# Which projections are split into heads and rests beside the attention of a two-layer decoder trunk: the convolution's inputs and gates take the place of the gated queries and keys, and the work hung on them is dealt anew

## The chip, the cores and the metric

One core of a Trainium2 chip runs the whole program: TensorE (PE) for matrix products, VectorE (DVE), ScalarE (ACT) and GpSimd (POOL) for the rest, and SyncE (SP), which only issues transfers here. The time is microseconds (us) on the device from the first to the last instruction with what lies around them. The value for a kernel is the median of its runs. The trace is of one execution.

## The reference

Two layers over 512 tokens of 1024 numbers. A layer is a token mixer, a cross-attention into a memory of 256 rows, and a mixture of 16 experts (two for each token). The change touches the mixer alone. It projects the normalised rows by one matrix, and three groups of heads work on the pieces:

```
h = rms_norm(x, norm_mix[l]);  z = h @ w_in[l]
(g_q, g_k, g_v, g_lr, g_r, d_q, d_k, d_v, i_q, i_k, i_w, c_u) = split(z)
# gated linear attention: 4 heads, 48 wide keys, chunks with an exact decay inside
log_a = log_sigmoid(g_lr @ wa2 + ba) / 16;  b = cumsum(log_a) in the chunk
attn[t,s] = sum_d q[t,d] k[s,d] exp(b[t,d] - b[s,d])   (s <= t)
o = attn @ v + (q exp(b)) @ state;  state = exp(b_last) state + (k exp(b_last - b))^T v
# sparse attention: 6 heads, each query keeps its 128 best causal keys by an indexer's score
# convolution: a, g = split(c_u);  y = a * sigmoid(g);  y = causal depthwise conv, 31 taps;
#              channel LayerNorm, swish
x = x + concat(o_gla * silu(g_r), o_dsa, o_conv) @ w_out[l]
```

## The kernel before

**Projections.** The 3,000 odd columns of `w_in` are loaded in nine chunks (`CHUNKS`) into three slots of the arena. `JOBS` lists the projections in the order in which PE makes them; a job of kind "T" gives 128 outputs by 512 tokens, one of kind "tok" 128 tokens by 384 outputs, and each is made of 8 units, one for each 128 rows of the contraction. Chunk 1 and chunks 2 to 5 (`SPLIT`) are computed from heads and rests: ACT copies the weights, rounded to the fast format, into a head (`chunk_head`), POOL writes the remainder (`chunk_rest`), and PE makes three fast products for a unit (`split_project`, line 708) in place of one slow product in full precision (line 726; line 729 for the 384 wide ones). The rows of h are split in the same way once.

**The steps.** After the indexer, 24 steps follow (4 query tiles by 6 heads, `STEPS`). In step n PE turns the probabilities of step n (line 848, 1 to 4 blocks), makes the logits of the next two steps (839) and the values of the last two (859) in even steps, and then does a share of the other work: units of projections, the decayed chunk keys turned ("kt", 740), state updates ("upd", 748), outputs of the gated heads ("o", 761 and 763). `work_of` deals these from the end of the list of jobs before the steps: `LENGTH` holds a time for each kind of unit, `attention` one for the step's own products, and the dealer keeps each step to a common pace, with one pace for the first `GATED` steps and another to step 21.

**The softmax ring.** DVE's step n begins with the inverse of the sum (`sum_inverse(n)`, line 1212) and the masked logits of the next step (`masked(n+1)`, 1207). ACT's step n normalises the probabilities (`normalise(n)`, 1044), takes the exponentials of the next step (1037), copies the turned probabilities (`turned`, 1062), and then copies out each job that ended in the step (`evacuate`, 955; 946 for updates, 934 and 938 for outputs). PE's turn of step n+1 waits for `normalise(n+1)`, which stands behind those copies on ACT and behind `sum_inverse(n+1)` on DVE.

**Levels.** The gated heads' matrix inside a chunk of 128 tokens (`AT`) is built in seven levels v = 0 to 6 (blocks of 1 to 64) and a diagonal. For each level DVE forms the differences of b (`differences`, 1233), ACT their exponentials (`level_decays`, 1075 and 1076), DVE multiplies by the queries (`level_queries`, 1241) and POOL by the keys (`level_keys`, 1356), PE makes the products (`level_products`, 788), and DVE, or ACT from level 5 on, merges them into `AT` (`merge`, 1257; `merge_blocks`, 1054). The diagonal (`diagonals`, 772) takes queries times keys from the third of three buffers `lev`, so `differences(2)` waits for it, and `differences(v)` waits for the products of level v-3. `LEV0`, the first step of the levels, comes from the step in which the last gated key is done.

**Around them.** When the last keys or gates are there, `decay_to_end` (1262) and `factors` (1266, 1269) make the factors of the state. The convolution is 62 operations of DVE (`conv_tap`, 1221 to 1224), spread over steps `FIRST_TAP` to 21 by `taps_spread`, which evens out `vector_us(n)`, DVE's other work as it is planned; DVE also makes ten rounds of the last tile's selection in steps 0 to 4. ACT takes the Sigmoid of the gates behind the copy of the last one (line 958), for which it loads another table of functions and then loads the first again.

## Time and profile before

| | us |
|---|---|
| median of 3 runs (lowest, highest) | 1549.1 (1540.87, 1553.7) |
| the profiled execution | 1541.7 |
| its span | 1539.5 |
| PE busy, DVE busy, ACT busy, POOL busy | 1427.3, 1163.9, 909.9, 552.0 |
| steps of layer 0, first turn to last value | 128.3 to about 297 |
| steps of layer 1 | 892.7 to about 1061 |

The profiled execution lies 2.2 us over its span and 7.4 us below the median of the runs. The steps of the two layers take some 168 us each, 22% of the span together; the rest is the indexer, cross-attention and above all the experts. A PE that is busy is not a PE at its peak: its busy time says that products follow each other, and its granted clock stands beside it.

### The profile page before, as it was taken

To read this page: it belongs to the slowest core of one execution; us is meant where nothing else is said; L and a number is where in the kernel's file an instruction comes from. 1 tells how busy PE (TensorE), PEld (TensorE's weight loads), DVE (VectorE), ACT (ScalarE), POOL (GpSimd) and SP (SyncE) were. 2 spreads that over 40 slices of the span, in tenths; PEclk is the share of its full clock that TensorE was granted. 3 is DMA by queue.
4 is the path that set the end of the run, shared out by engine and by line. 5 is a ranking of instruction groups with operands and counts; after the bars stand their busy time and mean duration, and the time that the engine had idled before them with its cause. 6 is when DMAs were issued, how large, how long until landed. Compare 5 with 4: busy or idle time off the path is not lost.

```text
span 1539.5 us, 20216 instructions
## 1 busy us (share of the span) xinstructions
PE 1427.3 (93%) x6710; PEld 1034.8 (67%) x6710; DVE 1163.9 (76%) x1658; ACT 909.9 (59%) x1346; POOL 552.0 (36%) x240
## 2 busy tenths in 40 slices
PE   7999998899899999999889999888998999999996
PEld 4687554457577878777556875544675778887773
DVE  4696589333569999999757965894335899999997
ACT  5643344553447787788475524446435588887781
POOL 2342332060005555554532413220600066555544
PEclk9999999999989999999999999999999999999998
DMA  6241601311328999999651421013221499999995
GB/s 227 89 110 42 217 1 55 137 57 37 128 110 302 399 398 399 398 399 399 227 197 42 109 74 76 1 55 137 57 89 77 152 340 399 399 399 398 398 399 196
DMA packets 151482, 312.71 MB, mean 203 GB/s; under 512 B 33158, under 2 KB 46380, under 8 KB 151228
## 3 DMA queue, kind: packets, MB, share of 16 engines
q1 hardware_dynamic: 140300, 271.39, 48.8%
q0 software_dynamic: 6624, 24.12, 4.2%
q10 hardware_dynamic: 4496, 16.40, 2.6%
q8 instruction: 36, 0.59, 0.2%
q14 instruction: 26, 0.21, 0.0%
HBM read 287.76 MB, written 29.50 MB: 206 GB/s over the span
## 4 chain that ended last, share of the span: by engine, by line
PE 45%; DVE 25%; DMA 17%; ACT 7%; issue 5%; DVEq 1%; POOL 0%; SPq 0%; POOLq 0%; ACTq 0%
PE ps L708 12%; DMA arena<-in_w_down 12%; DVE rest_w_down L1421 7%; PE ps L726 5%; PE ps L1498 4%; DVE mixr L1224 3%; DMA arena<-in_w_gate 3%; DVE rest_w_up L1421 3%; PE ps L1520 3%; DVE rest_w_gate L1421 2%; ACT head_w_down L1416 2%; PE ps L815 2%; DVE xg_rest L1434 2%; PE ps L1614 2%; PE ps L859 1%
## 5 line engine op out<-in xcount | busy, mean ns | idle before, releaser
L2084 POOL TENSOR_TENSOR rest_w_down<-arena,head_w_down 128x2048 fp32r<-128x2048 f32 x30 | 184.9, 6165 | 199.3 <-ACT head_w_down L1416 199.3
L1421 DVE TENSOR_TENSOR rest_w_down<-arena,head_w_down 128x2048 fp32r<-128x2048 f32 x30 | 148.3, 4944 | 16.9 <-ACT head_w_down L1416 16.8
L1421 DVE TENSOR_TENSOR rest_w_gate<-arena,head_w_gate 128x2048 fp32r<-128x2048 f32 x64 | 145.8, 2279 | 0.1
L1421 DVE TENSOR_TENSOR rest_w_up<-arena,head_w_up 128x2048 fp32r<-128x2048 f32 x64 | 143.5, 2281 | 0.1
L1416 ACT ACTIVATE head_w_gate<-arena 128x2048 fp32r<-128x2048 f32 x60 | 114.8, 1920 | 45.2 <-DMA arena<-in_w_gate 45.2
L1416 ACT ACTIVATE head_w_down<-arena 128x2048 fp32r<-128x2048 f32 x60 | 115.3, 1927 | 38.1 <-DMA arena<-in_w_down 37.4
L1416 ACT ACTIVATE head_w_up<-arena 128x2048 fp32r<-128x2048 f32 x64 | 121.8, 1946 | 8.3 <-DMA arena<-in_w_up 8.2
L1405 PE MATMUL ps<-head_w_gate,xg_head 128*128 128x512 f32 x256 | 104.1, 407 | 5.1 <-DVE xg_rest L1434 3.7
L1395 PE MATMUL ps<-head_w_down,he_head 128*128 128x512 f32 x240 | 99.5, 415 | 7.3 <-DVE rest_w_down L1421 4.3
L726 PE MATMUL ps<-hT,arena 128*128 128x512 f32 x224 | 101.7, 598 | 0.1
L1224 DVE SCALAR_TENSOR_TENSOR mixr<-arena,cf,mixr 128x512 f32<-128x512 f32 x120 | 97.6, 813 | 4.3
L1407 PE MATMUL ps<-head_w_gate,xg_rest 128*128 128x512 f32 x256 | 100.1, 391 | 0.0
L1406 PE MATMUL ps<-rest_w_gate,xg_head 128*128 128x512 f32 x256 | 100.0, 391 | 0.0
L1405 PE MATMUL ps<-head_w_up,xg_head 128*128 128x512 f32 x256 | 99.7, 390 | 0.0
L1407 PE MATMUL ps<-head_w_up,xg_rest 128*128 128x512 f32 x256 | 99.7, 389 | 0.0
L1406 PE MATMUL ps<-rest_w_up,xg_head 128*128 128x512 f32 x256 | 99.6, 389 | 0.0
L1397 PE MATMUL ps<-head_w_down,he_rest 128*128 128x512 f32 x240 | 94.1, 392 | 0.0
L1396 PE MATMUL ps<-rest_w_down,he_head 128*128 128x512 f32 x240 | 93.8, 391 | 0.0
L708 PE MATMUL ps<-hT_head,w_rest 128*128 128x512 f32 x224 | 90.0, 402 | 0.0
L2031 POOL DMA_INDIRECT xg<-hrows,slot_tok x2 | 4.9, 2436 | 236.4 <-DVE slot_tok L2002 236.4
L2077 POOL DMA_INDIRECT xg<-hrows,idx x28 | 76.4, 2728 | 21.0 <-POOL idx L2090 21.0
L1428 ACT ACTIVATE xg_head<-ps,cf 128x128 fp32r<-128x128 f32 x256 | 69.1, 379 | 23.0 <-PE ps L1688 16.4
(373 smaller groups left out, 3496.1 us busy)
## 6 DMA issues: line engine op xcount, KB each, us to landing
arena<-in_w_gate SPq DMA_DIRECT2D x64, 1024.0 KB, 10.5
arena<-in_w_up SPq DMA_DIRECT2D x64, 1024.0 KB, 11.4
arena<-in_w_down SPq DMA_DIRECT2D x64, 1024.0 KB, 10.7
arena<-in_w_in SPq DMA_DIRECT2D x10, 1536.0 KB, 6.6
yrows<-yb ACTq DMA_DIRECT2D x30, 512.0 KB, 6.3
arena<-in_w_in SPq DMA_DIRECT2D x4, 2048.0 KB, 8.6
x<-in_x SPq DMA_DIRECT2D x8, 512.0 KB, 13.5
arena<-in_w_in SPq DMA_DIRECT2D x16, 256.0 KB, 4.8
```

Source lines behind the costliest of these rows:

```text
L708: last = nc.tensor.matmul(o, lhs, rhs, start=(c == 0 and a == 0), stop=(c == KD - 1 and a == 2))
L726: last = nc.tensor.matmul(ps[n % 2][0:width, :], w[:, c, col:col + width], hT[:, c, :], start=(c == 0), stop=(c == KD - 1))
L1224: do(nc.vector.scalar_tensor_tensor(o, cin[:, i, j:j + S], convw[:, i, j:j + 1], o, ALU.mult, ALU.add))
L1395: nc.tensor.matmul(out, ah, bh, start=(c == 0), stop=False)
L1396: nc.tensor.matmul(out, ah, bl, start=False, stop=False)
L1397: last = nc.tensor.matmul(out, al, bh, start=False, stop=(c == n - 1))
L1405: nc.tensor.matmul(ps[q][:, :], xh[:, c, :], wh[q][:, c, :], start=(c == 0), stop=False)
L1406: nc.tensor.matmul(ps[q][:, :], xh[:, c, :], wl[q][:, c, :], start=False, stop=False)
L1407: last = nc.tensor.matmul(ps[q][:, :], xl[:, c, :], wh[q][:, c, :], start=False, stop=(c == KD - 1))
L1416: nc.scalar.activation(wh[q][:, part(q, j), :], raw[q][:, part(q, j), :], ACT.Copy).then_inc(s_head[q], 1)
L1421: nc.vector.tensor_tensor(wl[q][:, c, :], raw[q][:, c, :], wh[q][:, c, :].bitcast(F32), ALU.subtract).then_inc(s_split[q], 1)
L2084: nc.gpsimd.tensor_tensor(wl[2][:, c, :], raw[2][:, c, :], wh[2][:, c, :].bitcast(F32), ALU.subtract)\
```

## The change

The chunk of the convolution's inputs `ca` and gates `cg` is now the fifth and the chunk of the gated queries and keys the sixth, so the first is computed from heads and rests and the second in full precision. The times in `LENGTH` are swapped with them; the first pace covers 4 jobs over the first `GATED` = 4 steps, and the first output may come at step 19, not 16. The levels begin at step 8 (before: 4), the factors at steps 10 and 11 (8 and 9), the taps at step 4 (10: planned from 8 on, the first one fell to 10). The third level buffer lies in `sq`, and the wait for the last level product ahead of the second gate of `gr` falls away. In a step, PE makes two units, then the level products, then the other units; before, all units came first. The diagonal now closes PE's step `LEV0 + 2` (before: `LEV0 + 1`), the level products of v stand in step `LEV0 + 3 + v` (before: `+ 2`) and their merges in `+ 4` (before: `+ 3`).

```diff
     [(0, COL["dv"], AH * AD)],
+    [(0, COL["ca"], 2 * CC)],
     [(64 * h, COL["gq"] + GK * h, 64) for h in range(GH)] + [(256 + 64 * h, COL["gk"] + GK * h, 64) for h in range(GH)],
-    [(0, COL["ca"], 2 * CC)],
     [(0, COL["gv"], GH * GV)],
...
             csq = view(arena, up + 6656, 2, S)
-            lev = [view(mixg[:, :, :].rearrange("p h s -> p (h s)"), 1024 * i, 2, S) for i in range(2)] + [view(arena, up + 5120, 2, S)]
+            lev = [view(mixg[:, :, :].rearrange("p h s -> p (h s)"), 1024 * i, 2, S) for i in range(2)] + [sq[:, :, :]]
             lrT = view(arena, up + 11776, S, rows=RANK)
...
             BEFORE_STEPS = len(JOBS)
-            JOBS += [(5, P * i, P, "T", "gq", i) for i in range(2)] + [(5, 2 * P + P * i, P, "T", "gk", i) for i in range(2)]
-            JOBS += [(6, P * i, P, "T", "ca", i) for i in range(2)] + [(6, CC + P * i, P, "T", "cg", i) for i in range(2)]
+            JOBS += [(5, P * i, P, "T", "ca", i) for i in range(2)] + [(5, CC + P * i, P, "T", "cg", i) for i in range(2)]
+            JOBS += [(6, P * i, P, "T", "gq", i) for i in range(2)] + [(6, 2 * P + P * i, P, "T", "gk", i) for i in range(2)]
             JOBS += [(7, 0, GH * GV, "tok", "gv", i) for i in range(NT)]
...
-            LENGTH = dict(gq=0.7, gk=0.7, ca=0.87, cg=0.87, gr=0.87, gv=0.65, kt=0.6, upd=0.7, o=1.5)
-            GATED, LAST_FILLED, FIRST_O = 8, 22, 16
+            LENGTH = dict(ca=0.7, cg=0.7, gq=0.87, gk=0.87, gr=0.87, gv=0.65, kt=0.6, upd=0.7, o=1.5)
+            GATED, LAST_FILLED, FIRST_O = 4, 22, 19
...
                 i, h = STEPS[n]
-                return 0.3 * (i + 1) + (0.9 if 5 <= n < NLEV + 7 else 0.0)
+                return 0.3 * (i + 1) + (0.9 if 10 <= n < NLEV + 12 else 0.0)
...
             first, then = range(GATED), range(GATED, LAST_FILLED)
-            paces = [filler(("gq", "gk", "ca", "cg"), first) / len(first), filler(("gv", "kt", "gr", "upd", "o"), then) / len(then)]
+            paces = [filler(("ca", "cg"), first) / len(first), filler(("gq", "gk", "gv", "kt", "gr", "upd", "o"), then) / len(then)]
             work_of, left, spent = [], list(parts), 0.0
...
             LEV_BANK = (2, 7)
-            LEV0 = step_of(done("gk") - 1) + 1 if done("gk") > BEFORE_STEPS else 0
+            LEV0 = step_of(done("gk") - 1) - 1
...
                 return 2 * v + 1
-            FACTORED = step_of(done("cg") - 1) + 1
+            FACTORED = step_of(done("gk") - 1) + 1
             STATES = step_of(done("upd") - 1) + 1
...
                 us = 0.55 + 0.13 * (i + 1)
-                us += 2.5 if n == LEV0 + 2 else 0.0
-                us += 1.5 if 0 <= n - LEV0 - 3 < BY_BLOCKS else 0.0
+                us += 2.5 if n == LEV0 + 3 else 0.0
+                us += 1.5 if 0 <= n - LEV0 - 4 < BY_BLOCKS else 0.0
                 us += 0.8 if 0 <= n - LEV0 - 2 < NLEV else 0.0
...
                 sp.dma_start(one_head, A["heads"].rearrange("p (n c) -> p n c", c=P)).then_inc(sN["wor_in"], 16)
-                sp.wait_ge(sN["proj_done"], done("gk"))
+                sp.wait_ge(sN["proj_done"], done("cg"))
                 for t in range(NT):
...
                         values(n - 2)
-                    for job, c in work_of[n]:
+                    for job, c in work_of[n][:2]:
                         work(job, c)
-                    if n == LEV0 + 1:
+                    if 0 <= n - LEV0 - 3 < NLEV:
+                        level_products(n - LEV0 - 3)
+                    for job, c in work_of[n][2:]:
+                        work(job, c)
+                    if n == LEV0 + 2:
                         diagonals()
-                    if 0 <= n - LEV0 - 2 < NLEV:
-                        level_products(n - LEV0 - 2)
                     if n == MEAN:
...
                         return
-                    if name == "gr" and i:
-                        act.wait_ge(sN["lev_mm"], NLEV + 1)
                     src = ps[n % 2][0:width, :] if kind == "T" else ps[n % 2][:, 0:384]
...
                         level_decays(n - LEV0 - 1)
-                    if BY_BLOCKS <= n - LEV0 - 3 < NLEV:
+                    if BY_BLOCKS <= n - LEV0 - 4 < NLEV:
                         for e in range(2):
-                            merge_blocks(n - LEV0 - 3, e)
+                            merge_blocks(n - LEV0 - 4, e)
                     if n == FACTORED:
...
                     if v == 0:
-                        dve.wait_ge(sN["proj_out"], done("gk"))
+                        dve.wait_ge(sN["proj_out"], done("cg"))
                     if v >= 2:
...
                 def decay_to_end():
-                    dve.wait_ge(sN["proj_out"], done("cg"))
+                    dve.wait_ge(sN["proj_out"], done("gk"))
                     bc = halves(b, P // 2)
...
                         masked(n + 1)
-                    if n == LEV0 + 2:
+                    if n == LEV0 + 3:
                         merge(0)
-                    if 0 <= n - LEV0 - 3 < BY_BLOCKS:
+                    if 0 <= n - LEV0 - 4 < BY_BLOCKS:
                         for e in range(2):
-                            merge(PRODUCTS.index((n - LEV0 - 3, e)))
+                            merge(PRODUCTS.index((n - LEV0 - 4, e)))
                     if 0 <= n - LEV0 - 2 < NLEV:
...
                                                toep[:, h, 2 * P - P * near:2 * P], ALU.add), "bm_done")
-                    if n == LEV0 + 1:
+                    if n == step_of(done("cg") - 1) + 3:
+                        gp.wait_ge(sN["proj_out"], done("cg"))
+                        do(nc.gpsimd.memset(AT, 0.0), "at_zero")
+                    if n == LEV0 + 3:
                         gp.wait_ge(sN["proj_out"], done("gk"))
-                        do(nc.gpsimd.memset(AT, 0.0), "at_zero")
                         do(nc.gpsimd.tensor_tensor(lev[2], gq, gk, ALU.mult), "lev_k")
-                    if 0 <= n - LEV0 - 3 < NLEV:
-                        level_keys(n - LEV0 - 3)
+                    if 0 <= n - LEV0 - 4 < NLEV:
+                        level_keys(n - LEV0 - 4)
                     if n == STATES - 1:
```

PE around the diagonal. Line 772 is the diagonal, 788 the products of a level, 848 a turn (it opens a step), 726 and 729 units. Before, steps 5 to 7:

```order
L726 MATMUL ps<-hT,arena 128x512 x7
L772 MATMUL ps<-cf,arena 128x2 x8
L848 MATMUL ps<-cf,scratch 128x128 x2
L839 MATMUL ps<-scratch 128x256 x2
L859 MATMUL ps<-scratch 64x128 x2
L726 MATMUL ps<-hT,arena 128x512 x6
L788 MATMUL ps<-mixg 128x64 x16
```

PE now, steps 10 to 12:

```order
L729 MATMUL ps<-arena,hT 128x384 x6
L772 MATMUL ps<-cf,sq 128x2 x8
L848 MATMUL ps<-cf,scratch 128x128 x2
L729 MATMUL ps<-arena,hT 128x384 x2
L788 MATMUL ps<-mixg 128x64 x16
L729 MATMUL ps<-arena,hT 128x384 x5
L848 MATMUL ps<-cf,scratch 128x128 x3
```

The products of level 0 stood behind six units of their step and stand behind two now, with five behind them.

DVE at the same place: 1241 are the queries of a level, 1262, 1266 and 1269 the factors, 1224 taps, 1233 differences, 1257 the merge of the diagonal (128x2048) and of blocks. Before, from the differences of level 1 (step 5) to those of level 2 (step 6):

```order
L1233 TENSOR_TENSOR mixg<-arena 128x1024
L1212 RECIPROCAL small<-small 128x1
L1207 ISA scratch,small<-ps,scratch 128x256
L1207 ISA small 128x1
L1257 COPY_PREDICATED arena<-cmask,ps 128x2048
L1241 TENSOR_TENSOR mixg<-arena,mixg 128x512
L1233 TENSOR_TENSOR arena<-arena 128x1024
```

DVE now, steps 10 and 11:

```order
L1262 TENSOR_TENSOR arena<-arena 128x1024
L1224 SCALAR_TENSOR_TENSOR mixr<-arena,cf,mixr 128x512 x2
L1233 TENSOR_TENSOR sq<-arena 128x1024
L1212 RECIPROCAL small<-small 128x1
L1207 ISA scratch,small<-ps,scratch 128x384
L1207 ISA small 128x1
L1257 COPY_PREDICATED arena<-cmask,ps 128x2048
L1241 TENSOR_TENSOR mixg<-arena,mixg 128x256x2
L1266 TENSOR_TENSOR arena<-arena 128x1024
L1268 COPY ebl<-arena 128x8
L1269 TENSOR_TENSOR arena<-arena 128x1024
L1233 TENSOR_TENSOR mixg<-arena 128x1024
```

The merge of the diagonal and the two factors now stand in one step, and the differences of level 2 ahead of them, in the diagonal's own step.

PE behind the last gate. Before, the end of step 7 (behind the last unit of `cg`):

```order
L729 MATMUL ps<-arena,hT 128x384
L788 MATMUL ps<-mixg 128x64 x16
L848 MATMUL ps<-cf,scratch 128x128 x2
L839 MATMUL ps<-scratch 128x256 x2
L859 MATMUL ps<-scratch 64x128 x4
```

PE now, the end of step 3 (the second 726 row opens the work of step 4):

```order
L726 MATMUL ps<-hT,arena 128x512
L848 MATMUL ps<-cf,scratch 128x128
L839 MATMUL ps<-scratch 128x256 x2
L859 MATMUL ps<-scratch 64x128 x2
L726 MATMUL ps<-hT,arena 128x512 x6
```

Between the last unit of the gates and the next turn there was a unit and a level's products; there is one unit now.

## Rows read from the trace of the kernel before

**Rows 1.** Busy time by stage (us and instructions of each engine, granted clock, DMA): the steps
```profile
128.00:297.00 169.00, 150.65 (x815) 93.34 (x816) 121.35 (x200) 71.70 (x160) 39.46 (x35) 0.97 0.25 89
893.00:1061.00 168.00, 149.97 (x813) 93.05 (x813) 120.70 (x198) 70.69 (x156) 39.06 (x35) 0.97 0.17 63
```

**Rows 2.** Waits of PE in the steps (total us, times, longest): layer 0, layer 1
```profile
PE ps L848 <- ACT scratch L1044: 18.7, 10, 3.7
...
PE ps L848 <- ACT scratch L1044: 17.0, 9, 3.7
```

**Rows 3.** The chain of waits, layer 0 (start, us, what)
```profile
137.78 6.84 PE ps L708 x30
...
205.47 1.24 DVE arena L1233
```

**Rows 4.** Timeline of PE (start, us, what): units and a level's products
```profile
160.25 6.28 PE L726 MATMUL ps<-hT,arena 128*128 128x512 f32 x14
193.45 3.49 PE L729 MATMUL ps<-arena,hT 128*128 128x384 f32 x10
214.16 2.00 PE L788 MATMUL ps<-mixg 48*128 48x64 f32 x32
```

**Rows 5.** Timeline of PE: turns that waited, in brackets how long, and products behind them
```profile
191.86 0.44 PE L848 MATMUL ps<-cf,scratch 128*128 128x128 f32 x2 [0.88 <-ACT scratch L1044]
207.48 0.69 PE L848 MATMUL ps<-cf,scratch 128*128 128x128 f32 x2 [3.08 <-ACT scratch L1044]
208.10 1.65 PE L839 MATMUL ps<-scratch 64*128 64x384 f32 x4
209.68 1.12 PE L859 MATMUL ps<-scratch 128*64 128x128 f32 x8
...
223.45 0.92 PE L839 MATMUL ps<-scratch 64*128 64x384 f32 x4
224.29 0.66 PE L859 MATMUL ps<-scratch 128*64 128x128 f32 x8
270.73 0.66 PE L848 MATMUL ps<-cf,scratch 128*128 128x128 f32 x4 [3.66 <-ACT scratch L1044]
282.27 0.66 PE L848 MATMUL ps<-cf,scratch 128*128 128x128 f32 x4 [1.30 <-ACT scratch L1044]
289.48 1.12 PE L848 MATMUL ps<-cf,scratch 128*128 128x128 f32 x4 [3.49 <-ACT scratch L1044]
```

**Rows 6.** Timeline of DVE: differences, merges, factors, three taps
```profile
156.93 3.25 DVE L1233 TENSOR_TENSOR mixg<-arena 128x1024 f32<-128x1024 f32 x1
...
174.42 2.47 DVE L1257 COPY_PREDICATED arena<-cmask,ps 128x2048 f32<-128x2048 uint8 x1 [7.17 <-PE ps L772]
183.00 2.65 DVE L1257 COPY_PREDICATED arena<-cmask,ps 128x512 f32<-128x512 uint8 x2 [2.34 <-PE ps L788]
201.22 2.18 DVE L1266 TENSOR_TENSOR arena<-arena 128x1024 f32<-128x1024 f32 x1
203.64 1.80 DVE L1269 TENSOR_TENSOR arena<-arena 128x1024 f32<-128x1024 f32 x1
218.51 3.56 DVE L1224 SCALAR_TENSOR_TENSOR mixr<-arena,cf,mixr 128x512 f32<-128x512 f32 x3
```

**Rows 7.** Timeline of ACT: normalising 128 and 512 wide, a table load, a copied update
```profile
142.42 0.39 ACT L1044 ACTIVATE scratch<-scratch,small 128x128 f32<-128x128 f32 x1
189.06 1.28 ACT L958 ACT_TABLE_LOAD   x1
190.35 1.06 ACT L958 ACTIVATE arena<-arena 128x1024 f32<-128x1024 f32 x1
250.79 0.66 ACT L946 ACTIVATE arena<-ps 48x192 f32<-48x192 f32 x2
281.50 0.71 ACT L1044 ACTIVATE scratch<-scratch,small 128x512 f32<-128x512 f32 x1
```

**Rows 8.** Timeline of POOL: queries times keys for the diagonal
```profile
156.70 2.40 POOL L1372 TENSOR_TENSOR arena<-arena 128x1024 f32<-128x1024 f32 x1
```

## The prediction

> **What bounds the kernel now.** I read the busy time by stage first, because the change touches only the 24 steps of each layer. They take 169 us in layer 0 and 168 us in layer 1, with PE busy for 150.7 and 150.0 of them, DVE for 121 and ACT for 72 [rows 1]. So a step ends with PE, and what a new order can win is PE's idle time. The waits of PE name it: its turns waited 18.7 us for ACT's normalised probabilities, ten times, and in layer 1 17.0 us, nine times; the first wait, of 1.7 us, lies before that window [rows 2]. That is the stock, 18.7 us a layer. The change adds and removes no unit, tap, level or transfer, so PE's 150 us stay.
>
> The chain of waits then says who stands behind ACT. Until step 8 the chain is PE itself, ten split units in 6.84 us [rows 3]. After that, up to step 17 of layer 0, it runs mostly through DVE, taps and differences such as the one of 1.24 us. The timeline has three kinds of late turn [rows 5]: behind the Sigmoid (0.88 us), behind DVE's step with the factors (3.08), and behind copies on ACT of jobs that ended with the step (3.66 and 3.49 behind two outputs, 1.30 behind one copy). After the stall of 3.08 us the products crawl: logits 1.65 against 0.92 us, values 1.12 against 0.66 at the same shapes. The granted clock has fallen to its lower level, 1.2 GHz, and the stall costs 1.2 us more.
>
> **The change, part by part, for one layer.**
>
> *Split chunk and full chunk swapped.* Four jobs are still split and four are not: 32 units of 0.68 us [rows 3] and 32 of 0.87 to 0.90 (seven in 6.28 [rows 4]). The loads swap with them, on the same slots' turns, and the first split unit is needed no earlier. Zero; DVE idles in steps 0 to 3 either way.
>
> *What goes.* The stalls that came from DVE in steps 9 to 17: 3.08 behind the factors, and, of the 18.7, the rest once 1.7, 0.88, 3.66, 1.30 and 3.49 are taken off too, 4.6 us in four turns. DVE now makes 28 taps in steps 4 to 9, where it had waited for PE, for instance 7.17 us for the diagonal [rows 6]. The Sigmoid's 0.88 goes as well. And with no stall of 3 us there, the 1.2 us of slow clock.
>
> *What comes on ACT.* Every turn stands behind `evacuate` of the jobs that ended in the step before. One copy of 512 with nothing behind it on PE costs 1.30 us [rows 5], of which 0.71 is normalising 512 wide; 128 wide it takes 0.39 [rows 7], so 1.0. By the new deal:
> - turn 1: `ca` 0 fills step 0 to its last unit, 1.0. Turns 2 and 3: one unit of 0.68 covers it, 0.3 each.
> - turn 4: the old stall of 0.88 came behind a cover of a unit and a level's products, 0.70 and 2.00 [rows 4], so the chain from the last gate to the turn is 3.5 us. The cover is one unit of 0.87 now: 2.6.
> - turn 8: `gk` 0 ends step 7, 1.1. Turn 13: a `gv` ends step 12 and a tile's output is copied too, 1.5.
> - turn 17: two updates end step 16, each copied in two pieces, 0.66 for the first [rows 7], 1.4; and level 6 on PE waits in step 17 for ACT's merge of level 5, 0.6.
> - turn 19: `gr` 1 ends step 18, with a tile's output, 1.7.
> - turn 20: the outputs' 3.66 now have two full units behind them, 1.7, and no tile's output, about 0.5: 1.4.
>
> Together 11.9 us.
>
> *What comes on DVE.* `differences(2)` overwrites the buffer that the diagonal reads. The diagonal stood in step 5 and the differences in DVE's step 6; now both stand in step 10, the diagonal last. Turn 11 therefore waits for the differences, 1.24 [rows 3], the inverse and the normalising, some 0.7 with their signals: 2.0. It is a new wait; queued behind it on DVE is the whole ring.
> Step 11 then holds the merge of the diagonal, 2.47, both factors, 2.18 and 1.80 [rows 6], queries and differences: a microsecond more than the old step of the factors, which had two merges of blocks instead. PE's step 11 is longer by 1.4 us, two units. So the old 3.08 comes back as 2.7; I take 3.0, because PE's level 0 must also wait for the merge in the middle of the step.
>
> *What stays.* 1.7 at the first turn and 3.49 behind the last outputs.
>
> *The sum.* 11.9 + 2.0 + 3.0 + 1.7 + 3.5 = 22.1 us of stalls against 18.7, less 1.2 of clock: +2.2 a layer, +4.4 us for both. Nothing behind the steps gives it back, since the experts start when the mixer has ended. That makes the profiled execution 1541.7 + 4.4 = 1546. The median of the runs stands 7.4 above that execution, so the forecast for the median is 1549.1 + 4.4 = **1553.5 us**.
>
> *Bounds.* The job-end terms are bounded by the row of 1.30 and by zero, where the dealt work runs a little long. The two DVE terms can vanish (no stall in steps 10 to 12: 5 a layer less, so 1543.5) or grow (second rival).
>
> *A table load.* The row shows 1.28 us for the load, and the Sigmoid begins 1.29 after its start, with no gap [rows 7]. The Trainium skill, ScalarE: Activation LUTs, section What ACT_TABLE_LOAD costs, counts a drain of about 1.38 us with every load. By that rule turn 4 would wait 4.0 instead of 2.6 us, and the sum would be +7. The trace disagrees with it here, and the chain of 3.5 us is measured with everything in it.
>
> **The rivals.** A measurement of this kernel tells about 1% (15 us) from no change.
>
> *The reordering pays in full (faster).* If the new deal leaves DVE ahead everywhere and the copies on ACT find a cover, only 1.7, 2.6, 1.4 and 3.5 are left, 9.2 us instead of 18.7, and the clock's 1.2 goes too: -10.7 a layer, 1549.1 - 21 = 1528. For it: the old chain is DVE from step 9 to 17, and PE's work moves exactly there. Against it: turn 21 before had a job that ended its step and waited 1.30, and the new deal has four such places more. Its half (the DVE terms alone vanish, and some copies) is 1540. I give 0.08 to a gain of over 1% and 0.15 to one that stays within it.
>
> *The level ring goes round DVE and PE in one step (slower).* Now `differences(v)` waits for the products of level v-3 in PE's same step, and those wait for DVE's merges of level v-2 in that step. The loop is opening 0.8, merges 2.65, products 2.0, differences 1.24 and signals 0.3, some 7.0 us [rows 4, 6], against PE's own 5.7 to 7.7 us in steps 11 to 15: even. What decides is POOL. Differences that took 1.24 took 3.25 beside queries times keys on POOL, 2.40 long [rows 6, 8], and three taps took 3.56 instead of 2.4 beside key products. If POOL's key product and bias fall into each of these five steps at 2 us or more, the loop takes 8 to 9.4, some 5 us more a layer beyond the stalls counted, and two stalls of 3 us bring the low clock back, 2.4: about +9.5 a layer, 1549.1 + 19 = 1568. From 1.5 us of overlap a step on it decides. For it: the rows; against it: the same POOL operations stood beside the same steps before, and the whole stock was 18.7. Chance 0.12.
> The Trainium skill, SBUF — State Buffer, section Who interferes with whom, says that such a DVE operation with two inputs in SBUF is blocked whole while GpSimd reads SBUF. By it a step's overlap is all of POOL's 2 us, and this rival is the likelier case; the row of 3.25 agrees with it.
>
> *The forecast:* stalls change hands, 1545 to 1560, 0.65.
>
> **The numbers.** Range 1538 to 1567: half of the faster rival below, nearly all of the slower one above, and the runs before spread from 8 us under to 5 over their median. Faster by over 1% 0.08; within 1% 0.80, which is the forecast's 0.65 and the smaller gain's 0.15; slower by over 1% 0.12.
>
> **What would show it.** In the changed profile: PE's busy time in the steps unchanged at 150 us a layer; the waits of the turns at 20 to 24 us; a turn about 2.5 us late behind the Sigmoid, some 30 us into the steps; a turn 2 us late directly behind line 772; no turn more than 1 us late in steps 5 to 7; taps in steps 4 to 9. Wrong would be: turns that wait under 14 us in total (the copies are covered), or over 28 with DVE idle for line 788 in steps 12 to 15 (the ring).

## The result, and the profile after

The changed kernel takes 1556.5 us (median of 7 runs, 1555.5 to 1561.7), against 1543.9 (7 runs, 1539.0 to 1553.7) of the kernel before on the same chip: ratio 1.0076, with 95% interval 1.0053 to 1.0100. That is within 1%, as forecast, and the median lies in the range. But the loss is 12.6 us, where 4.4 were forecast, and its cause was only half forecast. That the median comes within 3.0 us of the 1553.5 forecast is luck: the forecast stood on a median of 1549.1 from three runs, which seven runs put at 1543.9.

The profiled execution took 1556.5 us (span 1554.0), against 1541.7 (span 1539.5) before. Measured from the first turn of a layer to its last one (turn 0 to turn 23), the steps grew from 166.05 to 173.03 us in layer 0 and from 166.22 to 170.47 in layer 1, together 11.2 of the 14.5 us by which the span grew. Some 3.0 more lie behind the last turn of layer 1 (480.6 to 483.6), a stretch that the change doesn't touch and that varies from 481.5 to 485.9 us over the experiments below.

Busy time by stage, in the changed kernel: the steps of layer 0 and of layer 1 from first to last turn, then a short stretch of each (window, length, busy us and instructions of PE, PEld, DVE, ACT, POOL, granted clock, DMA share, GB/s).

```profile
129.00:302.00 173.00, 154.86 (x794) 94.44 (x795) 115.30 (x196) 68.82 (x155) 36.51 (x35) 0.94 0.23 84
899.90:1070.40 170.50, 151.92 (x795) 92.41 (x796) 115.33 (x196) 68.72 (x155) 36.53 (x35) 0.96 0.17 60
...
208.90:219.30 10.40, 10.05 (x43) 6.53 (x42) 10.09 (x12) 2.04 (x5) 2.00 (x2) 0.51 0.00 0
983.80:987.10 3.30, 3.30 (x6) 1.69 (x6) 3.16 (x6) 0.17 (x1) 0.00 (x0) 0.50 0.00 0
```

The same stretches of the kernel before, turn to turn.

```profile
128.30:294.40 166.10, 148.74 (x795) 91.87 (x796) 119.70 (x196) 69.57 (x155) 39.40 (x35) 0.97 0.24 87
892.70:1058.90 166.20, 148.86 (x795) 92.05 (x796) 119.61 (x196) 69.50 (x155) 39.36 (x35) 0.97 0.17 62
```

PE holds as many instructions as before and is busy for 6.1 us more in layer 0 and 3.1 in layer 1. Its idle time grew by only 0.8 and 1.2 (17.4 to 18.1 and to 18.6). So most of the loss is not waiting: the same products took longer, and the granted clock says why, 0.94 and 0.96 for 0.97. For 10.4 us of layer 0 it was 0.51, that is 1.2 GHz, while PE was 97% busy. The other runs agree with this one execution: over the whole span the granted clock was 0.964 to 0.968 in the seven runs of the changed kernel, and 0.967 to 0.976 in 25 runs of the kernel before.

The waits of PE in the steps of layer 0 of the changed kernel (total us, times, longest) answer to [rows 2].

```profile
PE ps L848 <- ACT scratch L1044: 18.5, 12, 3.5
PE ps L859 <- ACT scratch L1062: 0.7, 1, 0.7
PE ps L788 <- ACT arena L1054: 0.6, 1, 0.6
PE ps L788 <- DVE arena L1257: 0.3, 1, 0.3
```

The turns wait 18.5 us where they waited 18.7 before, turn 0's 1.69 included in both; the levels add 0.9. The timeline of PE in the changed kernel answers to [rows 5]: turns 1, 4, 11 and 22 with their waits in brackets, and what follows turns 4 and 11.

```profile
137.99 0.33 PE L848 MATMUL ps<-cf,scratch 128*128 128x128 f32 x1 [0.98 <-ACT scratch L1044]
160.33 0.33 PE L848 MATMUL ps<-cf,scratch 128*128 128x128 f32 x1 [2.49 <-ACT scratch L1044]
...
161.29 0.69 PE L859 MATMUL ps<-scratch 128*64 128x128 f32 x4
161.92 6.68 PE L726 MATMUL ps<-hT,arena 128*128 128x512 f32 x12
...
207.72 0.44 PE L848 MATMUL ps<-cf,scratch 128*128 128x128 f32 x2 [2.12 <-ACT scratch L1044]
207.99 1.89 PE L729 MATMUL ps<-arena,hT 128*128 128x384 f32 x4
210.23 3.68 PE L788 MATMUL ps<-mixg 48*128 48x64 f32 x32 [0.35 <-DVE arena L1257]
213.84 6.09 PE L729 MATMUL ps<-arena,hT 128*128 128x384 f32 x10
...
296.95 0.66 PE L848 MATMUL ps<-cf,scratch 128*128 128x128 f32 x4 [3.50 <-ACT scratch L1044]
```

A level's products take 3.68 us where they took 2.00 [rows 4], and five units of 384 (x10, each unit leaves two records) take 6.09 where they took 3.49. Step 11, from turn 11 to turn 12, is 12.05 us long in layer 0. In layer 1, behind the same stall, the clock is down for 3.3 us only, and only from 5 us behind turn 11 on: the level's products still take 2.00 us, the five units 5.19.

```profile
978.73 0.44 PE L848 MATMUL ps<-cf,scratch 128*128 128x128 f32 x2 [2.13 <-ACT scratch L1044]
981.24 2.00 PE L788 MATMUL ps<-mixg 48*128 48x64 f32 x32 [0.78 <-DVE arena L1257]
983.17 5.19 PE L729 MATMUL ps<-arena,hT 128*128 128x384 f32 x10
```

There step 11 is 9.46 us long.

### The profile page after: what moved, and what is told of

It is laid out like the page before. It is cut to its first block, busy times and chain, and to the rows that moved or that the text cites. A ratio compares the mean times of both kernels' runs of the same rounds, so it can differ in the third digit from the quotient of the medians.

```text
span 1554.0 us, 20214 instructions
## 1 busy us (share of the span) xinstructions
PE 1441.8 (93%) x6710; PEld 1042.2 (67%) x6710; DVE 1157.0 (74%) x1658; ACT 908.9 (58%) x1346; POOL 546.3 (35%) x240
## 4 chain that ended last, share of the span: by engine, by line
PE 50%; DVE 20%; DMA 16%; ACT 7%; issue 5%; POOL 1%; DVEq 1%; POOLq 0%; SPq 0%; ACTq 0%
DMA arena<-in_w_down 13%; PE ps L708 12%; DVE rest_w_down L1423 8%; PE ps L726 6%; PE ps L1500 4%; DVE rest_w_up L1423 3%; PE ps L729 3%; PE ps L1522 3%; DVE rest_w_gate L1423 2%; ACT head_w_down L1418 2%; PE ps L815 2%; PE ps L788 2%; PE ps L1616 2%; DVE xg_rest L1436 2%; DMA arena<-in_w_gate 1%
## 5 line engine op out<-in xcount | busy, mean ns | idle before, releaser
L726 PE MATMUL ps<-hT,arena 128*128 128x512 f32 x224 | 106.3, 614 | 0.0
L1367 POOL TENSOR_TENSOR scratch<-sel,toep 128x256 f32<-128x256 f32 (+1 forms) x48 | 40.6, 846 | 149.6 <-DVE small L1207 135.7
## 6 DMA issues: line engine op xcount, KB each, us to landing
arena<-in_w_gate SPq DMA_DIRECT2D x64, 1024.0 KB, 10.4
```

Of the source, the lines that this page charges most:

```text
L726: last = nc.tensor.matmul(ps[n % 2][0:width, :], w[:, c, col:col + width], hT[:, c, :], start=(c == 0), stop=(c == KD - 1))
```

## The experiments

Theory A in them: the waits come as forecast, and those ahead of turns 4 and 11 also drop TensorE's clock, which makes the loss. "Steps" is turn 0 to turn 23, layer 0 / layer 1, in the one profiled execution. Ratios are to the kernel before, with 95% interval. That kernel was run anew on the chip of each set: its median was 1547.7 us beside the first four experiments, 1545.5 beside the next four and 1549.1 beside the last two. So kernels of different sets are compared by their ratios, not by their medians.

| kernel | steps, us | median, us (runs) | ratio |
|---|---|---|---|
| before | 166.05 / 166.22 | 1543.9 (7) | 1 |
| changed | 173.03 / 170.47 | 1556.5 (7) | 1.0076 [1.0053, 1.0100] |
| fillers in two waits | 168.73 / 168.23 | 1549.6 (10) | 1.0012 [0.9989, 1.0034] |
| diagonal first | 168.86 / 168.95 | 1547.7 (10) | 1.0001 [0.9980, 1.0023] |
| Sigmoid later | 168.30 / 166.65 | 1546.8 (10) | 1.0001 [0.9978, 1.0024] |
| taps late | 178.93 / 173.52 | 1564.0 (4) | 1.0115 [1.0082, 1.0147] |
| both moves | 164.59 / 166.32 | 1542.2 (12) | 0.9978 [0.9963, 0.9994] |
| ends covered | 164.30 / 163.01 | 1535.4 (6) | 0.9940 [0.9921, 0.9959] |
| before, with fillers | 166.51 / 166.47 | 1544.7 (10) | 0.9981 [0.9965, 0.9996] |
| ends covered, fillers | 159.79 / 161.48 | 1530.4 (6) | 0.9902 [0.9882, 0.9921] |
| units first | 184.01 / 177.06 | 1568.6 (4) | 1.0169 [1.0114, 1.0224] |
| more fillers | 159.78 / 161.49 | 1532.4 (6) | 0.9909 [0.9873, 0.9946] |

**Fillers in two waits.** Products of constants, two each time (x4, two records each), whose results nobody reads, go into the waits of turns 4 and 11.

```diff
                 for n in range(NS):
+                    if n in (4, 11):
+                        idle_products(2)
                     turn(n)
```

> The changed kernel with two products of ones (0.87 us each at full clock) put ahead of the turns of steps 4 and 11 in both layers, into an unused bank; nothing else. Theory A (the lost time is TensorE's clock: a stall of 2.1 to 2.5 us drops it to 1.2 GHz, and 4 to 10 us of products behind it run at half speed): the fillers run inside the waits of 2.49 and 2.12 us, the granted clock stays at 1.0 in steps 4 and 11, step 4 shrinks from 8.1 to about 6.3 us, step 11 from 12.05 (layer 0) and 9.46 (layer 1) to about 8.5 with 1 to 1.5 us of the gain coming back as a wait of turn 12 for DVE. In sum 7 to 9 us of the span go, ratio to before about 1.001 to 1.003. Theory B (DVE and PE hold each other up in the level ring, the clock is only a symptom): the steps keep their lengths, since turn 12 waits for DVE as long as PE saved; under 4 us go, nearly all of it in step 4.

Timeline of PE in this kernel, turns 4 and 11 of layer 0 with what follows them.

```profile
156.67 1.89 PE L401 MATMUL ps<-ones 128*128 128x512 f32 x4
159.33 0.33 PE L848 MATMUL ps<-cf,scratch 128*128 128x128 f32 x1 [0.77 <-ACT scratch L1046]
...
160.22 0.44 PE L859 MATMUL ps<-scratch 128*64 128x128 f32 x4
...
202.85 1.97 PE L401 MATMUL ps<-ones 128*128 128x512 f32 x4
205.12 0.44 PE L848 MATMUL ps<-cf,scratch 128*128 128x128 f32 x2 [0.30 <-ACT scratch L1046]
207.63 2.00 PE L788 MATMUL ps<-mixg 48*128 48x64 f32 x32 [0.78 <-DVE arena L1259]
209.56 5.18 PE L729 MATMUL ps<-arena,hT 128*128 128x384 f32 x10
```

No turn comes earlier: steps 3 and 10, which hold the waits, are 8.48 and 9.69 us long as in the changed kernel (8.47 and 9.69). But the products behind turn 4 go at full speed (0.44 for 0.69) and step 4 takes 6.51 us instead of 8.11; step 11 takes 9.46 instead of 12.05, and 8.87 in layer 1. So 4.3 of the 7.0 us that layer 0 had lost, and 2.2 of layer 1's 4.3, are clock behind these two stalls, shown by taking the idleness away and leaving the delay. Together that is 6.5 us of steps, a little under the 7 to 9 expected: a fall of a few us remained in step 11 of layer 0 (5.18 for the five units), and in layer 1, where none did, turn 12 waited 0.94 us.

**Diagonal first.** The diagonal's products go ahead of the remaining units of PE's step, so that DVE's differences are done when turn 11 wants its probabilities.

```diff
+                    if n == LEV0 + 2:
+                        diagonals()
                     for job, c in work_of[n][2:]:
                         work(job, c)
-                    if n == LEV0 + 2:
-                        diagonals()
```

> The changed kernel with the diagonal put behind the first two units of its step 10 instead of behind all six. Theory A: differences of level 2 no longer wait for it, the stall of 2.12 us ahead of turn 11 goes and with it the low clock of step 11: step 10 from 9.69 to about 7.5, step 11 from 12.05 and 9.46 to 7.5 to 9 (it may wait for the merge of the diagonal less, and turn 12 for the factors more), about 3 to 6 us a layer, 6 to 11 in all, and the median comes to within 0.3% of before. Theory B: the 2.1 us reappear as a wait of turn 12 or of the products of level 0 behind DVE, whose step 11 holds 9.5 us of work in any case: 0 to 3 us in all.

The wait ahead of turn 11 is gone: step 10 takes 7.51 us for 9.69, step 11 takes 8.71 for 12.05. Steps 3 to 5, with the Sigmoid's stall in them, stayed at 8.47, 8.11 and 5.26. Of the 5.5 us gained there in layer 0, 1.3 went again in step 22, 6.35 us for 5.07, behind the same stall of 3.50. Now, at full clock, turn 12 waits 1.09 us and level 0's products 0.52, 1.6 together, where 3.0 had been forecast for these steps and 0.35 came in layer 0 of the changed kernel: there PE crawled and DVE caught up.

**Sigmoid later.** ACT's table load and Sigmoid, which stood in `evacuate` right behind the last gate, go behind `turned` of the step that follows, past the probabilities that turn 4 wants.

```diff
-                    if name == "cg" and i == 1:
-                        act.wait_ge(sN["proj_out"], n + 1)
-                        nc.scalar.activation(csig, csig, ACT.Sigmoid).then_inc(sN["cg_ready"], 1)
...
                     turned(n)
+                    if n == step_of(done("cg") - 1) + 1:
+                        act.wait_ge(sN["proj_out"], done("cg"))
+                        nc.scalar.activation(csig, csig, ACT.Sigmoid).then_inc(sN["cg_ready"], 1)
```

> The changed kernel with the Sigmoid of the gates moved on ACT from behind the copy of the last gate to behind the copy of the turned probabilities of step 4, so that the turn of step 4 doesn't stand behind it. Theory A: turn 4 waits 0.3 to 0.4 us (the copy of the last gate alone) instead of 2.49, the clock stays up in step 4 (8.1 to 6.3 us), the first taps start a few us later and are made up in steps 5 to 9: 4 us a layer, about 8 in all. Theory B: DVE waits longer for the gates, its taps run into step 10 and the levels, and half of the gain is lost there: 4 us or less in all.

Timeline of ACT in this kernel.

```profile
156.69 0.60 ACT L955 ACTIVATE arena<-ps 128x512 f32<-128x512 f32 x1 [4.51 <-PE ps L708]
157.18 0.39 ACT L1041 ACTIVATE scratch<-scratch,small 128x128 f32<-128x128 f32 x1
159.35 1.28 ACT L1083 ACT_TABLE_LOAD   x1
160.64 1.06 ACT L1083 ACTIVATE arena<-arena 128x1024 f32<-128x1024 f32 x1
```

The probabilities now come 0.49 us after the copy begins, and the Sigmoid later. Steps 3 to 5 took 6.10, 6.95 and 5.79 us, 3.0 less than in the changed kernel. Turn 11 waited 2.13 us in both layers as before, but the clock fell less behind it: step 11 took 8.92 and 8.88 us. So this kernel gained more in its steps (4.7 and 3.8 us) than the move explains, because the same stall cost less this time.

**Taps late.** This undoes the part "taps dealt from the fifth step on": they begin in step 10.

```diff
-            FIRST_TAP, LAST_TAP, MEAN = step_of(done("cg") - 1) + 1, 21, 22
+            FIRST_TAP, LAST_TAP, MEAN = LEV0 + 2, 21, 22
```

> The changed kernel with the first tap planned from step 10 on, as the kernel before had it in effect, not from step 4: what the early taps are worth. DVE then has 92 us of work in steps 10 to 21 by the rows of before (30 us of it taps that stood in steps 4 to 9, in part even now covered), PE 79 us. Theory A: 3 to 6 us a layer longer than the changed kernel, all of it in waits of the turns 13 to 21 for DVE, 6 to 12 us in all. Theory B, in its form that DVE is not short of time here: no change within 3 us.

The waits of the turns in layer 0 are 20.5 us in 14 turns, for 18.5 in 12; turns 14 (0.77) and 16 (0.67) are new among them, and steps 15 and 17 take 7.64 and 8.95 us for 6.80 and 7.26. The steps are longer by 5.9 and 3.0 us, and the ratio goes from 1.0076 to 1.0115, some 6 us. Of the 5.9 only 2.0 are waits of the turns, where all of it had been expected: 0.6 of them at turn 11, 2.74 us for 2.12. The rest is mostly clock, and a part of that is chance: step 4 of layer 0 took 1.6 us more behind an unchanged wait, and steps 0 and 4 of layer 1 took 3.3 less. Without these the early taps are worth 4.3 and 6.3 us a layer. The kernel also shows the 2.49 us stall ahead of turn 4 once with a fall of the clock (step 4 of layer 0: 9.67 us) and once without (layer 1: 6.52). Timeline of PE in layer 1 of this kernel:

```profile
931.41 0.33 PE L848 MATMUL ps<-cf,scratch 128*128 128x128 f32 x1 [2.49 <-ACT scratch L1044]
...
932.67 5.42 PE L726 MATMUL ps<-hT,arena 128*128 128x512 f32 x12
```

**Both moves:** the diagonal first and the Sigmoid later, in one kernel.

> The changed kernel with both moves: the diagonal behind two units of step 10, and the Sigmoid behind the turned probabilities of step 4. Theory A (stalls and the clock that they drop): the gains of the two runs alone add, 2.2 + 3.3 us at the diagonal in layer 0 and 2.2 + 0.7 in layer 1, 2.9 and 3.8 at the Sigmoid: steps of 164 to 165 us in each layer against 166 before, so 2 to 4 us faster than before, ratio 0.997 to 0.999. Theory B (DVE and PE hold each other in the ring): the later taps and the earlier differences meet in steps 10 to 12, turn 12 waits 2 us or more, the steps stay at 167 or more, ratio 1.000 or above.

Timeline of PE in this kernel: turn 11, level 0 and turn 12 of layer 0.

```profile
201.76 0.38 PE L848 MATMUL ps<-cf,scratch 128*128 128x128 f32 x2
203.97 2.00 PE L788 MATMUL ps<-mixg 48*128 48x64 f32 x32 [0.53 <-DVE arena L1257]
210.47 0.55 PE L848 MATMUL ps<-cf,scratch 128*128 128x128 f32 x3 [1.08 <-ACT scratch L1041]
```

Turn 11 comes without a wait, all products are at full speed, and what is left of the DVE terms is 0.53 + 1.08. The steps of layer 0 are 8.4 us shorter than in the changed kernel, 1.5 shorter than before the change. Layer 1 gave 1.7 of it back in step 17, 8.95 us for 7.26, behind the same stall of 1.43.

**Ends covered.** To both moves it adds a rule of dealing: where a step ends with the last unit of a job, the first unit of the next job comes into it too. This acts in steps 0, 7 and 12.

```diff
                 work_of.append(mine)
+            for n in range(NS - 1):
+                units = lambda m: KD if JOBS[m][0] is not None else 1
...
+                    if (work_of[n] and ... and JOBS[work_of[n + 1][0][0]][3] in ("T", "tok")
+                            and work_of[n][-1][1] == units(work_of[n][-1][0]) - 1 and work_of[n + 1][0][1] == 0):
+                        work_of[n].append(work_of[n + 1].pop(0))
```

> As the run with both moves, and where a job's last unit closed a step and the next step opened with a fresh job, one unit of it is dealt ahead of the turn (behind steps 0, 7 and 12), so that the copy on ACT has a cover. Theory A: the waits of turns 1, 8 and 13 fall from 0.98, 1.08 and 1.46 by a unit each (0.7 to 0.9), by 2.2 us a layer together, no work added: 4 to 5 us less than with both moves, ratio about 0.995. Theory B: those turns then wait for DVE instead, no gain.

Timeline of PE in this kernel: turns 1, 13 and 14 of layer 0.

```profile
136.77 0.33 PE L854 MATMUL ps<-cf,scratch 128*128 128x128 f32 x1 [0.30 <-ACT scratch L1047]
218.20 0.55 PE L854 MATMUL ps<-cf,scratch 128*128 128x128 f32 x3 [0.82 <-ACT scratch L1047]
224.21 0.55 PE L854 MATMUL ps<-cf,scratch 128*128 128x128 f32 x3 [0.76 <-ACT scratch L1047]
```

The three waits, of turns 1, 8 and 13, fell from 0.98, 1.08 and 1.46 us to 0.30, 0.23 and 0.82: one unit of 0.68 to 0.87 us, moved from behind the turn to ahead of it, takes about its own length off the wait. But only two of the three are gained. The unit that step 12 took from step 13 leaves two behind the level's products there instead of three, and now turn 14, which had not waited, waits 0.76 us; step 13 is as long as before (6.01 us). So the gain is 1.5 us a layer and not the 2.2 expected. Layer 0 gave 1.2 of it back in step 22 (6.32 us for 5.08), and layer 1 shows 3.3 because its step 17 went at full clock this time (7.26 for 8.95).

**Before, with fillers.** The kernel before the change, with three products of constants in the stall of 3.08 us ahead of turn 10.

```diff
                 for n in range(NS):
+                    if n == 10:
+                        pe.wait_ge(sN["pt_out"], n)
+                        for _ in range(3):
+                            nc.tensor.matmul(ps[6], ones[:, :], ...)
                     turn(n)
```

> The kernel before with three products of ones ahead of turn 10, inside its stall of 3.08 us, in a bank that is free there; nothing else. It prices the clock in the kernel before. Theory A: the products behind that turn run at full clock, step 10 goes from 8.61 to about 7.3 us in each layer (1.2 to 1.3 us), 2.5 us in all. Theory B: no change, within 0.5 us a layer.

Timeline of PE in this kernel: fillers, turn 10, logits behind it, and turn 19.

```profile
205.26 2.85 PE L882 MATMUL ps<-ones 128*128 128x512 f32 x6
208.42 0.44 PE L848 MATMUL ps<-cf,scratch 128*128 128x128 f32 x2 [0.30 <-ACT scratch L1048]
208.79 0.92 PE L839 MATMUL ps<-scratch 64*128 64x384 f32 x4
...
270.24 0.92 PE L848 MATMUL ps<-cf,scratch 128*128 128x128 f32 x4 [3.66 <-ACT scratch L1048]
```

The logits take 0.92 us where they crawled at 1.65 [rows 5], and step 10 is 1.45 us shorter. But step 12 took 1.5 more, behind a wait of 0.65, of which 1.3 came back in step 13, since turn 14 then had nothing to wait for; and step 19 took 4.76 for 3.07, behind the stall of 3.66 that stood there all along. The steps are no shorter in total (166.51 for 166.05), so the 2.5 us that theory A expected are not seen in this execution, the slowest of the ten. The runs say 0.9981, some 3 us; where these come from is not shown.

**Ends covered, fillers.** The kernel with the ends covered, with such products also ahead of turn 0 (two) and turn 22 (three).

```diff
+                    if n == 0:
+                        for _ in range(2): nc.tensor.matmul(ps[6], ...)
+                    if n == 22:
+                        pe.wait_ge(sN["pt_out"], n)
+                        for _ in range(3): nc.tensor.matmul(ps[6], ...)
                     turn(n)
```

> As the run with covered job ends, and products of ones inside the stalls ahead of turn 0 (two, stall 1.69 us) and turn 22 (three, stall 3.50 us). Theory A: step 0 from 9.0 to 7.5 us and step 22 from 5.0 to 6.4 down to about 3.8: 2 to 3 us a layer more, 4 to 6 in all, ratio 0.991 to 0.993. It can lose where the clock is already low ahead of turn 0: the two products then take 3.5 us instead of 1.7 and delay the turn by 1.8. Theory B: no gain.

Timeline of PE in this kernel at turn 22, then its busy time by stage from turn 0 to turn 23.

```profile
280.55 2.75 PE L891 MATMUL ps<-ones 128*128 128x512 f32 x6
284.21 0.66 PE L854 MATMUL ps<-cf,scratch 128*128 128x128 f32 x4 [0.91 <-ACT scratch L1054]
```

```profile
127.80:287.60 159.80, 148.46 (x801) 89.47 (x801) 116.30 (x196) 69.32 (x155) 37.30 (x35) 1.00 0.24 86
883.90:1045.40 161.50, 150.15 (x801) 89.97 (x801) 116.27 (x196) 69.30 (x155) 37.26 (x35) 0.99 0.17 60
```

The turns come no earlier, but the clock is at 1.00 and 0.99. Step 22 takes 3.43 us for 6.32 in the kernel with the ends covered, step 0 takes 7.34 for 8.95. In layer 1 the same two steps gain 3.2 us, of which 1.7 are lost again in step 17, 8.95 us for 7.26. The ratio is 0.9902: this kernel beats both the one before and the changed one, with the change's own arrangement of projections.

**Units first.** All units of a step stand ahead of the level's products, which hands DVE its blocks late.

```diff
-                    for job, c in work_of[n][:2]:
+                    for job, c in work_of[n]:
                         work(job, c)
                     if 0 <= n - LEV0 - 3 < NLEV:
                         level_products(n - LEV0 - 3)
-                    for job, c in work_of[n][2:]:
-                        work(job, c)
```

> The changed kernel with PE's order inside a step undone: all units first, then the level's products, as before; the offsets of levels and merges stay. It tells what placing the products behind two units is worth, and whether the wait that cost a stall at the diagonal is a general one. The differences of level v wait for the products of level v-3 in the same step. Theory A (a turn stalls where DVE has to wait for the end of PE's step, as at turn 11): turns 12 to 15 wait 1.5 to 2 us each in place of 0 to 1.5, and the clock falls behind some of them: 5 to 10 us a layer longer than the changed kernel, ratio to before about 1.015 to 1.02. Theory B (the ring through DVE binds in the changed kernel as it is): little change, under 2 us a layer, since the products' place then makes no difference to a loop that DVE sets.

Turns 12, 13 and 15 in this kernel, and after them the differences of DVE ahead of turns 13 and 14 of the changed kernel.

```profile
215.59 0.55 PE L848 MATMUL ps<-cf,scratch 128*128 128x128 f32 x3 [2.24 <-ACT scratch L1042]
227.41 0.90 PE L848 MATMUL ps<-cf,scratch 128*128 128x128 f32 x3 [2.24 <-ACT scratch L1042]
...
251.38 0.90 PE L848 MATMUL ps<-cf,scratch 128*128 128x128 f32 x3 [2.24 <-ACT scratch L1042]
```

```profile
225.23 1.23 DVE L1233 TENSOR_TENSOR mixg<-arena 128x1024 f32<-128x1024 f32 x1 [5.39 <-PE ps L788]
233.24 1.23 DVE L1233 TENSOR_TENSOR sq<-arena 128x1024 f32<-128x1024 f32 x1 [2.64 <-PE ps L788]
```

DVE waits for line 788 in the changed kernel too, 5.39 and 2.64 us, but its differences are done before the turn wants its probabilities. With the units first they come last, turns 12 to 15 wait 2.24 each, the products at turns 13 to 15 take 0.90 for 0.55, and the steps grow by 11.0 and 6.6 us. It is the wait of turn 11 four times over: between the last of the level's products and the turn stand the differences (1.23 us), the inverse and the normalising, 2.24 us in all, with nothing for PE to do. It is not the whole loop of the slower rival, in which the level's products wait for DVE's merges: in this kernel they wait for DVE nowhere in layer 0. In the changed kernel the units behind the level's products cover the 2.24 us: four in step 12, three in step 13. With two left there, in the kernel with the ends covered, turn 14 waited.

**More fillers.** One product of constants more ahead of each of turns 17, 19 and 20 of the previous best kernel.

```diff
+                    if n in (17, 19, 20):
+                        pe.wait_ge(sN["pt_out"], n)
+                        nc.tensor.matmul(ps[6], ...)
```

> As the run with covered job ends and products of ones at turns 0 and 22, and one more such product in each of the stalls ahead of turns 17, 19 and 20 (1.43, 1.68 and 1.43 us). Theory A: those stalls dropped the clock in one layer of two in the runs so far (step 17 at 8.95 in place of 7.26 us), so about 1.7 us go in all and nothing is lost: within 0.1% of that run, ratio about 0.989 to 0.990. Theory B: the products delay the turns, 0.5 us each, 3 us longer.

Their waits fell to 0.57, 0.82 and 0.57 us, and nothing else moved: step 17 of layer 1 takes 8.96 us as without them (8.95), the steps 159.78 and 161.49 for 159.79 and 161.48. The 1.7 us that theory A expected there were not seen, and the 3 us longer of theory B neither. What drops the clock in that step stays open.

## Why the prediction held, and where it failed

- **The turns behind job ends, right.** Forecast and measured (layer 0), in us: turn 1 1.0 and 0.98; turns 2 and 3 0.3 and 0.30; turn 8 1.1 and 1.08; turn 13 1.5 and 1.46; turn 17 1.4 and 1.43, with level 6's 0.6 and 0.59; turn 19 1.7 and 1.68; turn 20 1.4 and 1.43; turn 22 3.5 and 3.50. The method, a chain's length from an old row less the new cover, works to 0.1 us where the chain is on ACT.
- **Behind the Sigmoid and the differences, right.** 2.6 for turn 4 came as 2.49, 2.0 for turn 11 as 2.12. The rule of the Trainium skill (ScalarE: Activation LUTs, What ACT_TABLE_LOAD costs) had given 4.0 for turn 4; the trace disagrees with it here, and in the changed kernel, too, the Sigmoid starts right behind the load, 1.30 us after its start.
- **"PE's 150 us stay", and "with no stall of 3 us there, the 1.2 us of slow clock" goes: the step that failed.** The clock term was -1.2 us a layer; PE's busy time grew by 6.1 and 3.1 instead. I had tied the fall of the clock to one stall and its length, because one row showed it. The two shorter new stalls dropped it as well, as the fillers show. The rows of before held the warning: behind 3.49 us the turn took 1.12 us for 0.66, behind 3.66 it did not slow [rows 5]. And behind turn 0's stall of 1.69 us the kernel before crawls as well, as two rows of PE show, one split product at the lower clock and one at full:

```profile
130.10 0.63 PE L708 MATMUL ps<-hT_rest,w_head 128*128 128x512 f32 x1
136.36 0.39 PE L708 MATMUL ps<-hT_head,w_rest 128*128 128x512 f32 x1
```

- **"I take 3.0" for steps 11 and 12: wrong, and partly for that same reason.** The measured waits were 0.35 us in layer 0 and 0.78 in layer 1, since a slow PE lets DVE catch up; at full clock they are 1.6. Even so the term had been sized 1.4 too large. It cancelled some of the missing clock term, which kept the total nearer than its parts; that is luck, too.
- **"No turn more than 1 us late in steps 5 to 7", taps in steps 4 to 9:** right. The sum counted 4.6 us of waits in four turns as gone. The changed kernel has no wait at a turn that isn't named above, and with the taps late 2.0 us of waits come back.
- **The waits "at 20 to 24 us" and PE's busy time "unchanged":** both signs missed. The turns wait 18.5 us, and PE is busy for 154.9 and 151.9 us from turn 0 to turn 23, where it was 148.7 and 148.9.
- **The faster rival** did not come by itself. Its gain, 1528 for 1549.1 or a ratio of 0.986, is what the kernel with covered ends and fillers comes near (0.990), but only once the diagonal and the Sigmoid are moved, three job ends covered and two stalls filled.
- **The slower rival** did not come. DVE does idle for line 788, but the turns' waits stay under 28 us, and of the level's products only those of level 0 wait for DVE (0.35 us). No row stood behind its 5.7 to 7.7 us for PE's own steps: without waits of turns, steps 12 to 15 are 8.1, 6.0, 8.7 and 6.8 us long, which leaves DVE more time. The overlap with POOL that it named is real, but falls in step 10, on a factor, where DVE had time. Timelines of DVE and of POOL in the changed kernel:

```profile
196.42 3.25 DVE L1262 TENSOR_TENSOR arena<-arena 128x1024 f32<-128x1024 f32 x1
...
205.70 1.22 DVE L1233 TENSOR_TENSOR sq<-arena 128x1024 f32<-128x1024 f32 x1 [4.11 <-PE ps L772]
```

```profile
195.75 2.85 POOL L1374 TENSOR_TENSOR sq<-arena 128x1024 f32<-128x1024 f32 x1 [13.12 <-ACT arena L955]
```

The two-input operation of DVE takes 3.25 us beside POOL's 2.85, and 1.22 alone (line 1262 itself took 1.22 in the kernel before, and the differences of the same shape do here), which agrees with the Trainium skill, SBUF — State Buffer, Who interferes with whom.

In short: the stalls were forecast as 22.1 us a layer and measured as 19.5 in layer 0 (18.5, 0.6 and 0.35), the clock as -1.2 and measured as some +6 and +3.

## What to carry to other kernels

Where a change only moves stalls, add their lengths, and then ask for each new one whether PE's products behind it will go at the lower clock. For a single stall no run here lets one say so beforehand: in these kernels stalls of 1.4 to 3.7 us cost between nothing and 3.3 us on top (step 11: 12.05 us, and 8.71 at full clock without the stall). What cures it is to have the engine that feeds the next product do that first (a table load, a block of differences behind it), to put one unit of other work between the end of a job and the product that waits (and not to take it from where it covers another chain, as at turn 14), and to fill what idle time is left with products that nobody reads.

## What the hardware did that I had not expected

- The same stall does not always drop the clock. 2.49 us ahead of turn 4 gave a step 4 of 8.11, 8.18 and 9.67 us, and once 6.52; 2.12 ahead of turn 11 gave 12.05, 9.46 and, with the Sigmoid later, 8.92 and 8.88; 3.66 ahead of turn 19 gave 3.07 and 4.76; 1.43 ahead of turn 17 gave 7.26 and 8.95; 3.50 ahead of turn 22 gave from 3.43 to 6.40.
- The clock stayed down although PE worked: 10.4 us at 0.51 with PE 97% busy (above).
- Filling one stall moved a fall to later ones (the kernel before, with fillers; there the fall in step 12 stands behind a wait of only 0.65 us), so the gain of a filler is read from the whole stretch, not from its step.
